# Turning the expert rows of the last layer: gathered fp32 rows against one-hot products of three bf16 parts kept on chip

## The reference, cut to what matters

```python
scores = jax.nn.sigmoid(h @ router_w)
_, idx = lax.top_k(scores + router_bias, TOP_K)          # 8 of 64
gates = s_sel / jnp.sum(s_sel, axis=-1, keepdims=True) * ROUTED_SCALE
...
xb = h_pad[tok]                                           # the rows of one expert's tokens
hid = jax.nn.silu(xb @ w_gate[e]) * (xb @ w_up[e])        # 1024 -> 256
y = hid @ w_down[e]                                       # 256 -> 1024
routed = jax.ops.segment_sum(y * gate, buf_tok)
shared = (jax.nn.silu(h @ sh_gate) * (h @ sh_up)) @ sh_down
out = rms_norm(x + gate_row * (routed + shared), final_norm)
```

## Time and profile before

| | us |
|---|---|
| median of 3 runs (1794.94 to 1799.71) | 1795.64 |
| the profiled execution's own time | 1800.63 |
| its span in the profile | 1798.8 |
| PE busy | 1650.9 (92%) |
| DVE busy | 582.2 (32%) |
| ACT busy | 300.6 (17%) |
| POOL busy | 205.4 (11%) |

### The profile page before, as it was taken

How to read it: one execution, slowest core, us unless ns; L and a number is a source line. 1 busy time by engine, 2 the same in 40 slices (tenths; PEclk the granted TensorE clock), 3 DMA queues, 4 the chain that set the end, 5 groups by cost and what they waited for, 6 DMA issues and landing times. The chain is left out here.

```text
span 1798.8 us, 23072 instructions
## 1 busy us (share of the span) xinstructions
PE 1650.9 (92%) x8479; PEld 722.1 (40%) x8479; DVE 582.2 (32%) x1354; ACT 300.6 (17%) x685; POOL 205.4 (11%) x197
## 2 busy tenths in 40 slices
PE   5999998999999999999998699988799899798898
PEld 2544444554333333434343244454333233233232
DVE  2232774464222122222211553375322122112122
ACT  2102452230111111111111121173100000000001
POOL 0300442001111111111110000030000000000000
PEclk9999999989999999999999799999899999999899
DMA  8714983065999999999999952303999999999995
GB/s 320 224 49 164 353 286 131 1 267 208 422 401 406 420 415 406 407 411 400 417 414 407 372 215 77 110 1 106 399 391 397 421 418 414 419 419 420 413 415 208
DMA packets 124833, 563.95 MB, mean 314 GB/s; under 512 B 17866, under 2 KB 23449, under 8 KB 74160
## 3 DMA queue, kind: packets, MB, share of 16 engines
q1 hardware_dynamic: 106336, 515.40, 71.7%
q0 software_dynamic: 17248, 43.62, 6.4%
q10 hardware_dynamic: 1136, 3.43, 0.5%
HBM read 553.10 MB, written 26.83 MB: 322 GB/s over the span
## 5 line engine op out<-in xcount | busy, mean ns | idle before, releaser
L1886 PE MATMUL ps<-wb,pool 128*32 128x512 f32 (+2 forms) x2608 | 494.9, 608 | 20.4 <-issue 20.2
L1886 PEld LDWEIGHTS ps<-wb,pool 128*32 128x32 f32 (+2 forms) x2608 | 160.0, 126 | 310.5 <-issue 310.5
L1900 DVE TENSOR_TENSOR ffn_hid<-ffn_sg,ps 128x256 f32<-128x256 f32 x71 | 29.9, 421 | 565.5 <-ACT ffn_sg L1894 565.5
L1930 PE MATMUL ps<-pool,ffn_hidT 128*32 128x512 f32 (+2 forms) x584 | 164.1, 597 | 3.4 <-DVE ffn_hidT L1915 2.3
L1930 PE MATMUL ps<-hT,ffn_hidT 128*32 128x512 f32 (+2 forms) x680 | 156.5, 597 | 5.4 <-DVE ffn_hidT L1915 3.0
L1787 POOL DMA_INDIRECT pool<-h_rows,ffn_index x71 | 72.5, 1021 | 619.2 <-DVE ffn_index L1837 322.6
L2661 PE MATMUL ps<-wb,hT 128*128 128x512 f32 x320 | 141.1, 602 | 1.9 <-issue 1.6
L1894 ACT ACTIVATE ffn_sg<-ps 128x256 f32<-128x256 f32 x71 | 27.2, 383 | 568.1 <-PE ps L1886 568.1
L1958 PE MATMUL ps<-x_res,rw 128*128 128x512 f32 x224 | 114.1, 613 | 0.0
L1930 PE MATMUL ps<-sh_wd,ffn_hidT 128*32 128x512 f32 (+2 forms) x272 | 100.1, 596 | 2.5 <-DVE ffn_hidT L1915 1.8
L1850 PE MATMUL ps<-const,pool 128*128 128x128 f32 x568 | 91.0, 284 | 8.2 <-DMA pool<-h_rows,ffn_index 6.1
(11 more groups left out here) (343 smaller groups left out, 1759.7 us busy)
## 6 DMA issues: line engine op xcount, KB each, us to landing
wb<-in_expert_w_gate_dram SPq DMA_DIRECT2D x106, 1024.0 KB, 16.7
wb<-in_expert_w_up_dram SPq DMA_DIRECT2D x106, 1024.0 KB, 20.4
pool<-in_expert_w_down_dram SPq DMA_DIRECT2D x52, 1024.0 KB, 19.3
hT<-in_expert_w_down_dram SPq DMA_DIRECT2D x52, 1024.0 KB, 17.4
wb<-in_ada_w_dram SPq DMA_DIRECT2D x20, 2048.0 KB, 10.5
sh_wd<-in_expert_w_down_dram SPq DMA_DIRECT2D x24, 1024.0 KB
wb<-in_diff_w_in_dram SPq DMA_DIRECT2D x6, 2048.0 KB, 17.6
mix_yr<-y_rows SPq DMA_DIRECT2D x6, 2048.0 KB, 15.3
```

What stands on the lines that cost most here:

```text
L1886: mm = nc.tensor.matmul(core.ps[lo:lo + width, gu_bank(n), :], xT[:, n % 2, k, lo:lo + width], w[:, k], start=k == 0, stop=k == KD - 1, sk ...
L1900: nc.vector.tensor_tensor(hid[:, n % 2, :], sg[:, n % 2, :], core.ps[:, gu_bank(n), F:2 * F], ALU.mult).then_inc(hid_ready, 1)
L1930: mm = nc.tensor.matmul(core.ps[lo:lo + width, down_bank(half), :], hidT[:, n % 2, k, lo:lo + width], wd_at(q % DR, half, k), start=k == 0 ...
```

## The change

In the last layer the rows aren't stored or gathered. After the turning back, each half (128 tokens by 512 features) is split on chip into three bf16 parts: ACT casts the fp32 values to bf16 (part 0), DVE subtracts part 0 from them in fp32, ACT casts the rest (part 1), DVE writes what is left as part 2. The parts are written with the features reordered to `[k][c]` and take the place of `hrow` and of the gather buffers. A round's turned rows are then products: for each of 8 feature blocks, for each of 2 token tiles, for each of 3 parts, the part block (128 tokens by 128 features, bf16) is the loaded operand and the batch's one-hot matrix (128 tokens by 128 slots, bf16) the moving one; six products add up in one PSUM block. That is 48 products a round where 8 transposes stood. POOL has nothing left to do in this layer. `dve_info` leaves out the indices. Since the one-hot matrix is now read until a round's rows are made, `dve_hot` of the next batch moves from the first round of a batch to the third (behind a wait on `xb_turned`), and `pe_info`/`dve_info` to the fourth. Ahead of round 0 the placement sums move up between the two shared gate-up products, the turning back is done in two parts around the first half of the second gate-up, and the two halves of round 0 are made around the shared down product of tile 0. The first layer keeps its code.

```diff
+        def act_split(act, n):
+            act.wait_ge(turned, n + 1)
+            nc.scalar.copy(part_view(0, n), split_view(core.ps[:, back_bank(n), :])).then_inc(taken, 1)
+            act.wait_ge(rest1, n + 1)
+            nc.scalar.copy(part_view(1, n), split_view(rest[:, n % 2, :])).then_inc(cast1, 1)
+        def dve_split(dve, n):
+            dve.wait_ge(taken, n + 1)
+            if n >= 2:
+                dve.wait_ge(parts_ready, n - 1)
+            nc.vector.tensor_tensor(split_view(rest[:, n % 2, :]), split_view(core.ps[:, back_bank(n), :]), part_view(0, n),
+                                    ALU.subtract).then_inc(rest1, 1)
+        def dve_split_end(dve, n):
+            dve.wait_ge(cast1, n + 1)
+            nc.vector.tensor_tensor(part_view(2, n), split_view(rest[:, n % 2, :]), part_view(1, n),
+                                    ALU.subtract).then_inc(parts_ready, 1)
+        def pe_make_x(pe, n, half):
+            if n == 0:
+                pe.wait_ge(parts_ready, 2 * NT)
+                pe.wait_ge(scratch_free, 1)
+            pe.wait_ge(hot_ready, n // BATCH + 1)
+            if half == 1:
+                pe.wait_ge(xa_ready, n + 1)
+            elif n >= 1:
+                pe.wait_ge(xb_ready, n)
+            m = n % BATCH * UNITS
+            for k in range(4 * half, 4 * half + 4):
+                for i in range(NT):
+                    hot = onehot[:, i, m:m + UNITS, :].rearrange("p u s -> p (u s)")
+                    for b in range(3):
+                        mm = nc.tensor.matmul(core.ps[:, x_bank(half), (k % 4) * P:(k % 4 + 1) * P], parts[:, b, i, k, :], hot,
+                                              start=i == 0 and b == 0, stop=i == NT - 1 and b == 2, skip_group_check=True)
+            mm.then_inc((xa_turned, xb_turned)[half], 1)
...
@@ gpsimd
+                if last:
+                    return
...
@@ scalar
                 for n, (i, half) in enumerate(back):
+                    if last:
+                        act_split(act, n)
+                        continue
...
@@ vector
-                dve_shared_hidden(dve, 0)
-                dve_shared_hidden(dve, 1)
+                if last:
+                    dve_split(dve, 0)
+                    dve_split(dve, 1)
...
                 dve_hot(dve, 0)
+                if last:
+                    for n in range(2, 2 * NT):
+                        dve_split_end(dve, n - 2)
+                        dve_split(dve, n)
+                    dve_shared_hidden(dve, 0)
+                    for n in range(2 * NT - 2, 2 * NT):
+                        dve_split_end(dve, n)
+                    dve_shared_hidden(dve, 1)
...
-                    ahead = n % BATCH == 0 and b < plan.batches
+                    ahead = n % BATCH == (BATCH - 1 if last else 0) and b < plan.batches
...
                         dve_gated_y(dve, n, 0)
+                        if n % BATCH == BATCH - 2 and b < plan.batches:
+                            dve_hot(dve, b)
                         dve_back_hot(dve, n)
...
@@ tensor
+                if last:
+                    for n in range(NT):
+                        turn_back(n)
+                    place_rows()
+                    pe_shared_gate_up(pe, 1, 0, KD // 2)
+                    for n in range(NT, 2 * NT):
+                        turn_back(n)
+                    pe_shared_gate_up(pe, 1, KD // 2)
...
                 for i in range(NT):
-                    if i == NT - 1:
+                    if last:
+                        pe_make_x(pe, 0, i)
+                    elif i == NT - 1:
...
-                            pe_turn(pe, n + 1, 0)
+                            pe_make_x(pe, n + 1, 0)
...
-                            pe_turn(pe, n + 1, 1)
+                            pe_make_x(pe, n + 1, 1)
```

More of the change, by code:

```diff
@@ L1615, in feed_forward @@
         gu_in = r.gu_in
-        gathered = [st.pool_sem(f"gathered{i}") for i in range(RING)]
+        if not last:
+            gathered = [st.pool_sem(f"gathered{i}") for i in range(RING)]
         if not last:
             r.scattered = scattered = [st.pool_sem(f"scattered{i}") for i in range(2)]
-        gathers, scatters = st.sem("gathers"), st.sem("scatters")
+        if not last:
+            gathers, scatters = st.sem("gathers"), st.sem("scatters")
         hot_ready, info_sum, index_ready, own = (st.sem(n) for n in ("hot_ready", "info_sum", "index_ready", "own"))
@@ L1693, in pe_shared_turn @@
             pe.wait_ge(sh_hid, i + 1)
-            if i == 0:
+            if i == 0 and not last:
                 pe.wait_ge(taken, 2 * NT)
+            elif i == 0:
+                pe.wait_ge(vgT_ready, 1)
             else:
@@ L1810, in pe_info @@
             pe.wait_ge(hot_ready, b + 1)
+            if b == 0 and last:
+                pe.wait_ge(rest1, 2 * NT)
             if b >= 1:
@@ L1857, in dve_take_x @@
                 dve.wait_ge(gu_ready, n - 1)
+            if n == 0 and last:
+                dve.wait_ge(parts_ready, 2 * NT)
             nc.vector.tensor_copy(xT[:, n % 2, 0:4, :].rearrange("p k c -> p (k c)"),
@@ L2109, in fb_dve @@
                                               ALU.add)
+                if last:
+                    nc.vector.tensor_scalar(fb_hot16[:, i, :], slots, place[:, i, bass.ds(e, 1)], None, ALU.is_equal)
             ins.then_inc(fb_hot_ready, 1)
@@ L2150, in fb_pe @@
             mm.then_inc(fb_summed, 1)
[L2151 to L2154, removed]
+            if last:
+                for k in range(KD):
+                    for i in range(NT):
+                        for part_of in range(3):
+                            mm = nc.tensor.matmul(core.ps[:, fb_x_bank + k // 4, (k % 4) * P:(k % 4 + 1) * P],
+                                                  parts[:, part_of, i, k, :], fb_hot16[:, i, :],
+                                                  start=i == 0 and part_of == 0, stop=i == NT - 1 and part_of == 2,
+                                                  skip_group_check=True)
+            else:
+                pe.wait_ge(fb_in, 16 * n + 16)
+                for k in range(KD):
+                    mm = nc.tensor.transpose(core.ps[:, fb_x_bank + k // 4, (k % 4) * P:(k % 4 + 1) * P], xs[:, 0, k:D:KD],
+                                             core.c("ident"))
             mm.then_inc(fb_x_turned, 1)
@@ L2397, in _ @@
                     b = n // BATCH + 1
-                    ahead = n % BATCH == 0 and b < plan.batches
+                    ahead = n % BATCH == (BATCH - 1 if last else 0) and b < plan.batches
                     if n >= 1 and not last:
                         dve_y(dve, n - 1)
-                    if ahead:
+                    if ahead and not last:
                         dve_hot(dve, b)
@@ L2471, in _, with turn_back @@
                 pe_shared_gate_up(pe, 0, part)
-                for n, (i, half) in enumerate(back):
+                def turn_back(n):
+                    i, half = back[n]
                     if n >= 2:
-                        pe.wait_ge(taken, n - 1)
+                        pe.wait_ge(rest1 if last else taken, n - 1)
                     for k in range(4):
@@ L2478, in _, with place_rows @@
                     mm.then_inc(turned, 1)
[L2479 to L2488, removed]
+                def place_rows():
+                    pe.wait_ge(mask_u_ready, 1)
+                    for i in range(NT):
+                        for j in range(i + 1):
+                            mm = nc.tensor.matmul(core.ps[:, v_bank(i), (i % 2) * U:(i % 2 + 1) * U],
+                                                  core.c("before") if j == i else core.c("ones"), mask_u[:, j, :],
+                                                  start=j == 0, stop=j == i)
+                    mm.then_inc(placed_u, 1)
+                if last:
+                    for n in range(NT):
[5 more added lines that the diff above has]
+                    pe_shared_gate_up(pe, 1, KD // 2)
+                else:
+                    for n in range(2 * NT):
+                        turn_back(n)
+                    pe.wait_ge(taken, 2 * NT - 1)
+                    pe_shared_gate_up(pe, 1)
+                    place_rows()
                 pe_shared_turn(pe, 0)
```

52 lines of the change are left out of this document (37 added, 15 removed).

## The result

The changed kernel takes 1804.12 us (median of 12 runs, 1802.28 to 1812.04) against 1795.65 us before (12 runs): a ratio of 1.0048, 95% interval 1.0035 to 1.0062. It is 8.5 us slower where 7.6 us of gain were forecast. The time lies at the upper end of the range given, the direction is wrong.

A forecast was written before the change was run, and what follows sets the result against it. DMA was taken to bound the rounds, PE close behind. Silu of round 0 at 1300.1 plus 27 steps of 473.3 (420.3 + 47.0 + 6) ends 7.6 us earlier: 1795.64 - 7.6 = 1788 us, range 1779 to 1805.

The forecast's parts named there:

- The bound of the rounds: Last layer's rounds: bound by DMA with PE close behind; removing gathers and row store gives at most 25 us.
- The new products: Each round: 48 products at 0.0545 us, load hidden, replace 8 transposes; 1.74 us longer a round, 47.0 over 27 steps.
- Rival A: Rounds: operand loads aren't hidden, 0.079 us a product; about 1815 us, 19 us slower than before; chance 0.13.
- rival C: Rounds: DMA stays the bound, PE keeps up, lead at the start larger; gain up to 15 us, 1780; chance 0.12.
- The waits in the rounds: Rounds: short waits for weights, 1 to 3 us at rounds 17 and 23; 6 us put down, bounds 0 and 15.
- the start decides: Rounds: DMA and PE are level, so DMA's lead of some 30 us at round 0 decides.
- Ahead of round 0: Before round 0's gate-up: new chain, split costed like plain rows, starts it 8.0 us earlier; bounds 0 and +5 us.
- The moved one-hot: `dve_hot` (1.23 us) at its later place is covered by PE's products: costed at nothing, at most 7 us.
- Rival B: Load partly shows, or split and first x slow, or moved `dve_hot` shows: +4 to +14 us, 1792 to 1802; chance 0.25.

## Why the prediction was wrong, step by step

- **The bound of the rounds**: right. DMA set the pace and PE was close behind: taking the gathers alone out gave 18 us, within the 25 that this side could give, and left 22.7 us of waits for weights.
- **The new products**: right. They advance at (1.50 - 0.219) / 23 = 0.0557 us, the load hidden; 0.0545 was taken. The Trainium skill's 81 ns (TensorE: Matmul & The Clock Gate, section Back-to-back issue gap) is not what this stream does. A round grew from 15.5 to 17.36 us, 1.86 where 1.74 was forecast. Rival A falls, and rival C with it, since PE is busy without a gap.
- **The waits in the rounds**: 6 us were put down; there is one of 2.0 us at round 17 as forecast, with a granted clock of 0.58 from 1609 to 1613 us behind it. The wait forecast at round 23 didn't come, and why is open. The sentence that "the start decides" is not borne out: the kernel with plain writes starts round 0 18.1 us earlier behind the first load and still waits only 2.3 us, and the one with the fp32 rest at a stride, which starts nearly as late as the changed kernel (54.4 us), waits 2.2 us. The 27 steps were forecast at 473.3 us and took 474.9.
- **Ahead of round 0**: this is the step that failed, and in it the sentence "These writes are strided bf16; I cost them like the plain rows, bounds 0 and +5 us in all". 40.5 us were forecast from the first load to silu 0 (1300.1 - 1259.6) and 55.5 came: 15.0 us more, twice the gain forecast. In it were some 3 us of waiting for the split and 1.9 us for the clock. Twelve of the sixteen operations took 2.4 to 2.8 us and four 1.02 instead of 0.54 and 0.69, in a chain that ACT and DVE pass back and forth with both PSUM banks held, so PE waited 4.5, 6.5 and 4.0 us, and at the lower clock the work behind those waits took some 4.4 us more than in the kernel with plain writes. With that cost taken away and nothing else, the same interval is 37.3 us, 3.2 better than forecast, and the kernel is faster than before. The upper bound of 5 us was not worked out from a row, though the trace of before had some that warn (groups by line from 1255 to 1300 us; busy us, mean ns of one). The first casts 112 values from SBUF into bf16 cells 8 B apart. The second writes such cells from PSUM, and the third 224 plain fp32 values from PSUM.

```profile
L2353 DVE CAST ffn_slot_info<-pool 128x112 bf16<-128x112 f32 x6 | 1.4, 325 | 0.1
...
L2345 DVE TENSOR_SCALAR ffn_slot_info<-ps 128x112 bf16<-128x112 f32 x2 | 0.7, 461 | 0.0
...
L2340 DVE TENSOR_SCALAR pool<-ps 128x224 f32<-128x224 f32 x1 | 0.4, 391 | 0.0
```

  From PSUM, half the values take longer: 4.1 ns a value against 1.7. The casts from SBUF take 2.9. These are whole durations of short operations, fixed part included, and another stride, so they are no price for 512 values. But at 2.9 to 4.1 ns the twelve writes would be 1.5 to 2.1 us each, 11 to 18 us more in all than as plain rows, an estimate. A bound of that size would have covered the sign of the forecast.
- **The moved one-hot**: right to cost it at nothing. PE's waits have no line for it.
- **Rival B** named the slow split among its causes, but at 4 to 14 us on the forecast for several small things together; it was one thing at 15.

By these steps: -7.6 forecast, +15.0 ahead of round 0, +1.6 in the rounds, +1.5 from the untouched part of that execution, make the 10.4 us between the two profiled executions, but for rounding.

## What to carry to other kernels

When a change trades transfers for work of an engine that is nearly as busy, price both sides: they can nearly cancel, as 18.5 and 20.5 us did here. The sign is then decided elsewhere, here in the serial stretch ahead of the loop, where the 18.1 us of the plain writes came out at the end in full. An operation whose output has another type and another order than any row of the trace has no price yet: give it the widest bound of the sum, and when reordering is needed put the stride on the fp32 read and let bf16 values be written side by side. Before giving up a change that came out slower, look which of its waits are new: here they were 15 us in three lines, and turning two loops round removed all but 1.2.

## What the runs showed of the hardware that was not expected

- ACT and DVE both write bf16 values 16 B or 256 B apart at about a quarter of the speed: on ACT 2.47 us (256 B) and 2.51 (16 B) against 0.62 for 512 values per partition, on DVE, which also reads a bf16 operand at the same stride, 2.44 and 2.49 against 0.68. It doesn't hold down to every stride: casts of 112 values into cells 8 B apart took 0.31 to 0.35 us.
- The subtraction that reads bf16 at a stride and writes fp32 lies between: 1.02 us at 256 B and 1.09 at 16 B, against 0.69. Writing its fp32 values at a stride of 256 B too adds next to nothing (1.04); such a write without the strided read was not run. An fp32 read from PSUM at 32 B costs nothing extra: 0.69 us on DVE and 0.58 on ACT with it and without.
- The Trainium skill (SBUF — State Buffer, section Door 1: The DMA port swizzle) says that accesses pay when they leave a line of 16 B, and names 8 bf16 or 4 fp32 as what can be strided for free. The runs disagree on the first: bf16 writes at a stride of 8 elements are as slow as at 128. For fp32 they only bound the price: 64 elements apart, and so a new line each time, the write adds 0.02 us beside the strided read.
- A load of a 128x128 bf16 block into PE at a stride of 16 B takes 147 ns instead of 98 and lengthens a stream of 128-column products from 0.0557 to 0.0615 us each: of the extra 49 ns some 6 show.
